# State-space heads: the state product for two heads at once, and an order of VectorE and ScalarE work around it

## What is computed

```python
    cb = jnp.einsum('bclgn,bcsgn->bcgls', c_c, b_c)
    y_diag = jnp.einsum('bcgjls,bcsgjp->bclgjp', cb[:, :, :, None] * decay, xdt)
    states = jnp.einsum('bclgn,bclgjp->bcgjpn', b_c, xdt * decay_to_end[..., None])
    # prev: the states passed on from chunk to chunk
    decay_from_start = jnp.exp(a_cs).transpose(0, 1, 4, 2, 3)
    y_off = jnp.einsum('bclgn,bcgjpn->bclgjp', c_c, prev) * decay_from_start[..., None]
    y = (y_diag + y_off).reshape(bsz, n_chunks * SSD_CHUNK, SSD_D_INNER)[:, pad:]
    y = y + xs.astype(f32) * jnp.repeat(d_skip.astype(f32), SSD_HEAD_DIM)
```

## Time and profile before

| | us |
|---|---|
| median of 3 runs | 2684.39 |
| lowest and highest | 2682.53, 2685.54 |
| profiled execution, own time | 2682.57 |
| its span, first to last instruction | 2680.8 |
| PE busy | 2585.4 (96%) |
| DVE busy | 1276.8 (48%) |
| ScalarE busy | 994.2 (37%) |
| POOL busy | 934.8 (35%) |

### The profile page before, as it was taken

The page is one execution under the profiler, slowest core; times in us unless marked ns, Lnnn a source line. Parts: engine busy times, 40 slices in busy tenths (PEclk is TensorE's granted clock), DMA queues, the critical chain, the costliest instruction groups (busy, mean ns, idle before and its releaser), DMA issues.

```text
span 2680.8 us, 36115 instructions
## 1 busy us (share of the span) xinstructions
PE 2585.4 (96%) x15112; PEld 2229.1 (83%) x15112; DVE 1276.8 (48%) x1729; ACT 994.2 (37%) x1520; POOL 934.8 (35%) x382
## 2 busy tenths in 40 slices
PE   7999999899999998899999999999997999999999
PEld 5777777677777787799999899999995887788887
DVE  6454452264454415788888543211235776522211
ACT  3333333343333334244454423322334565333321
POOL 3344344334334342222333234344432001344443
PEclk9999999999999999899999999999998999999999
DMA  4233233223333331212212123223221000233332
GB/s 138 89 99 103 89 106 91 75 84 110 89 98 106 94 95 47 63 56 64 64 58 62 49 86 100 89 87 95 87 75 56 17 17 25 70 111 94 94 96 87
DMA packets 61329, 215.66 MB, mean 80 GB/s; under 512 B 8176, under 2 KB 8560, under 8 KB 61168
## 3 DMA queue, kind: packets, MB, share of 16 engines
q1 hardware_dynamic: 57248, 202.05, 25.2%
q10 hardware_dynamic: 3920, 11.31, 1.3%
...
## 4 chain that ended last, share of the span: by engine, by line
PE 88%; DVE 7%; ACT 2%; issue 2%; DMA 1%; POOL 0%; DVEq 0%; ACTq 0%
PE psum L379 75%; PE psum L473 1%; PE psum L483 1%; PE psum L670 1%; PE psum L961 1%; PE psum L995 1%; PE psum L673 1%; PE psum L391 1%; PE psum L625 1%; DMA sb_w_raw<-in_weights 1%; DVE sb_cdec L2000 1%; PE psum L959 1%; PE psum L978 1%; PE psum L934 1%; DVE sb_scale L1577 1%
## 5 line engine op out<-in xcount | busy, mean ns | idle before, releaser
L353 POOL TENSOR_TENSOR sb_w_lo<-sb_w_raw,sb_w_hi 128x1024 fp32r<-128x1024 f32 x377 | 933.6, 2479 | 1718.5 <-ACT sb_w_hi L1115 1718.5
L379 PE MATMUL psum<-sb_h_hi,sb_w_hi 128*128 128x512 f32 (+1 forms) x2648 | 818.5, 351 | 48.1 <-DVE sb_h_lo L1586 32.3
L379 PE MATMUL psum<-sb_h_lo,sb_w_hi 128*128 128x512 f32 (+1 forms) x2648 | 795.7, 342 | 0.0
L379 PE MATMUL psum<-sb_h_hi,sb_w_lo 128*128 128x512 f32 (+1 forms) x2648 | 792.8, 341 | 0.0
L1115 ACT ACTIVATE sb_w_hi<-sb_w_raw 128x1024 fp32r<-128x1024 f32 x377 | 395.8, 1055 | 605.5 <-PE psum L379 455.2
L379 PEld LDWEIGHTS psum<-sb_h_hi,sb_w_hi 128*128 128x128 f32 x2648 | 459.8, 191 | 121.3 <-issue 32.7
L379 PEld LDWEIGHTS psum<-sb_h_lo,sb_w_hi 128*128 128x128 f32 x2648 | 458.8, 190 | 60.3 <-issue 4.4
L379 PEld LDWEIGHTS psum<-sb_h_hi,sb_w_lo 128*128 128x128 f32 x2648 | 459.0, 191 | 56.3
L379 PE MATMUL psum<-sb_mix_hi,sb_w_hi 128*128 128x264 f32 (+1 forms) x1424 | 417.8, 339 | 10.3 <-POOL sb_w_lo L353 5.6
L379 PE MATMUL psum<-sb_mix_lo,sb_w_hi 128*128 128x264 f32 (+1 forms) x1424 | 412.1, 335 | 0.0
L379 PE MATMUL psum<-sb_mix_hi,sb_w_lo 128*128 128x264 f32 (+1 forms) x1424 | 410.8, 334 | 0.0
...
## 6 DMA issues: line engine op xcount, KB each, us to landing
...
```

What stands on the lines that cost most here:

```text
L353: e.tensor_tensor(g.w_lo[:, u % 4, :], g.w_raw[:, u % 2, :], g.w_hi[:, u % 4, :].bitcast(F32), ALU.subtract).then_inc(S["w_lo"], 1)
L379: mm = e.matmul(g.psum[0:m, at + b, 0:wd], w[:, slot, P * i:P * i + m], xs[:, tile, c:c + wd], start=first and n == 0, stop=last and n == 2)
```

## The change

- `pe_ssd_a` runs once for two heads: the first head's rows go to partitions 0 to 63, the second's to 64 to 127, from position Q = 88 on. There are four instructions, of 176 and 264 columns for each head, of 64 weights.
- New `pe_ssd_state_y`: for two heads at once, the states of the pair (128 columns of `state` as weights) by C itself, five products of 88 columns. It is done beside unit 0 after seven of its eight blocks, and beside unit 2 after four. It waits for the states, the second time for `skip`.
- `pe_ssd_y` keeps only `xdt` by `part`; it waits for `state_y`.
- New `act_ssd_decays_from_start`: the exponential into `cdec`, once for a pair; for the second pair it comes after the norm's `act_rsqrt` beside head 1.
- New `dve_ssd_state_y`: `cdec` times the product in PSUM, then `xs` times the scalar plus that, into the group's output for positions 88 on. `dve_ssd_skip` is now two instructions: the first 88 positions as before, and for the others a sum of output and PSUM. DVE no longer multiplies by C (L2000).
- `pe_ssd_mask` of odd heads waits for the exponentials of the head before.
- Order on DVE: `dve_ssd_skip` of the first pair beside head 1, weights of head 2 behind the first tap of conv 1, the second state product behind its second tap, weights of head 3 ahead of the low parts and of conv 2. In the last group the low parts come ahead of the weights of head 3.
- Order on ScalarE: the split beside head 0 comes ahead of that head's decays; the one beside head 1 behind the second exponential of the pair.

The names of the new semaphores in the list SIGNALS are left out here.

```diff
@@ -627,25 +627,42 @@
     mm.then_inc(S["states_sum"], 1)
 
 
-def pe_ssd_a(g, e, grp, h):
-
-    S = g.S
-    n = HG * grp + h
-    if h == 0:
+def pe_ssd_a(g, e, grp, c):
+
+    S = g.S
+    n = HG * grp + 2 * c
+    if c == 0:
         e.wait_ge(S["bt2"], grp + 1)
     else:
         e.wait_ge(S["decay2"], n)
-    for half in range(2):
-        mm = e.matmul(g.flat(6 * 512 + 248 + HALF * half, HALF), g.sel[0:96, n:n + 1].to_broadcast([96, P]),
-                      g.rows[0:96, HALF * half:HALF * half + HALF], start=True, stop=True)
+    for h in range(2):
+        by, rows = g.sel[0:96, n + h:n + h + 1].to_broadcast([96, 64]), slice(64 * h, 64 * h + 64)
+        e.matmul(g.flat(6 * 512 + 248 + Q, HALF - Q)[rows], by, g.rows[0:96, Q:HALF], start=True, stop=True)
+        mm = e.matmul(g.flat(7 * 512, HALF)[rows], by, g.rows[0:96, HALF:L], start=True, stop=True)
     mm.then_inc(S["a_row"], 1)
 
 
+def pe_ssd_state_y(g, e, grp, c):
+
+    S = g.S
+    if c == 0:
+        e.wait_ge(S["state"], STEPS_OF_STATE * (grp + 1))
+    else:
+        e.wait_ge(S["skip"], 2 * grp + 1)
+    for j in range(1, NC):
+        mm = e.matmul(g.flat(4 * 512 + 248 + Q * j, Q), g.state[:, j - 1, P * c:P * c + P],
+                      g.ct[:, grp % 2, Q * j:Q * j + Q], start=True, stop=True)
+    mm.then_inc(S["c_state"], 1)
+
+
 def pe_ssd_mask(g, e, grp, h):
 
     S = g.S
     n = HG * grp + h
-    e.wait_ge(S["decay1"], n + 1)
+    if h % 2 == 0:
+        e.wait_ge(S["decay1"], n // 2 + 1)
+    else:
+        e.wait_ge(S["decay2"], n)
     for half in range(2):
         e.matmul(g.flat(6 * 512 + 248 + HALF * half, HALF)[0:Q], g.sel[0:96, n:n + 1].to_broadcast([96, Q]),
                  g.rows[0:96, HALF * half:HALF * half + HALF], start=True, stop=False)
@@ -659,19 +676,12 @@
 
     S = g.S
     n, row = HG * grp + h, 64 * (h % 2)
-    if h == 0:
-        e.wait_ge(S["state"], STEPS_OF_STATE * (grp + 1))
-    if h == 2:
-        e.wait_ge(S["skip"], 2 * grp + 1)
+    if h % 2 == 0:
+        e.wait_ge(S["state_y"], 2 * grp + h // 2 + 1)
     e.wait_ge(S["weighted"], n + 1)
-    e.wait_ge(S["c_dec"], n + 1)
     for j in range(NC):
-        out = g.flat(4 * 512 + 248 + Q * j, Q)[row:row + 64]
-        mm = e.matmul(out, g.xdt[0:Q, j, 64 * h:64 * h + 64], g.part[0:Q, h % 2, Q * j:Q * j + Q],
-                      start=True, stop=j == 0)
-        if j:
-            mm = e.matmul(out, g.state[:, j - 1, 64 * h:64 * h + 64],
-                          g.cdec[:, h % 2, Q * (j - 1):Q * j], start=False, stop=True)
+        mm = e.matmul(g.flat(4 * 512 + 248 + Q * j, Q)[row:row + 64], g.xdt[0:Q, j, 64 * h:64 * h + 64],
+                      g.part[0:Q, h % 2, Q * j:Q * j + Q], start=True, stop=True)
     mm.then_inc(S["y_part"], 1)
 
 
@@ -755,12 +765,23 @@
                 pe_ssd_out(g, e, h, 0, range(4))
             else:
                 pe_ssd_out(g, e, h - 2, 1, range(3))
-            if h < HG - 1:
-                pe_ssd_a(g, e, grp, h + 1)
+            if h == 0:
+                if not last:
+                    pe_ssd_unit(g, e, grp + 1, 0, range(4, 7))
+                else:
+                    pe_ssd_out(g, e, 0, 0, range(4, 7))
+                pe_ssd_state_y(g, e, grp, 0)
+                rest = range(7, 8)
+            else:
+                rest = range(4, 8)
+            if h == 1:
+                pe_ssd_a(g, e, grp, 1)
+            elif h == 2:
+                pe_ssd_state_y(g, e, grp, 1)
             if not last:
-                pe_ssd_unit(g, e, grp + 1, h, range(4, 8))
+                pe_ssd_unit(g, e, grp + 1, h, rest)
             elif h < 2:
-                pe_ssd_out(g, e, h, 0, range(4, 8)).then_inc(S["unit"], 1)
+                pe_ssd_out(g, e, h, 0, rest).then_inc(S["unit"], 1)
             else:
                 pe_ssd_out(g, e, h - 2, 1, range(3, 6))
             if h == 0 and grp:
@@ -1277,17 +1298,26 @@
         act_ssd_squares_high(g, e, grp - 1)
 
 
+def act_ssd_decays_from_start(g, e, grp, c):
+
+    S = g.S
+    e.wait_ge(S["a_row"], 2 * grp + c + 1)
+    if grp:
+        e.wait_ge(S["with_skip"], 2 * (grp - 1) + c + 1)
+    e.activation(g.cdec[:, c, :], g.flat(6 * 512 + 248 + Q, L - Q), ACT.Exp).then_inc(S["decay1"], 1)
+
+
 def act_ssd_decays(g, e, grp, h):
 
     S = g.S
     n = HG * grp + h
-    e.wait_ge(S["a_row"], n + 1)
-    if n >= 2:
-        e.wait_ge(S["y_part"], n - 1)
     at = 6 * 512 + 248
     if n == 0:
         e.wait_ge(S["dt_v"], DT_ALL)
-    e.activation(g.cdec[:, h % 2, :], g.flat(at + Q, L - Q), ACT.Exp).then_inc(S["decay1"], 1)
+    if n >= 2:
+        e.wait_ge(S["y_part"], n - 1)
+    if h == 0:
+        act_ssd_decays_from_start(g, e, grp, 0)
     if h == 2 and grp:
         act_ssd_high(g, e, grp - 1)
     e.wait_ge(S["masked"], n + 1)
@@ -1315,11 +1345,15 @@
     for grp in range(GROUPS):
         e.preload_act_table_set("natural_log_exp_and_others")
         for h in range(HG):
+            if h == 0:
+                act_split(g, e, U_SSD + GROUP * (grp + 1) + LEAD)
             act_ssd_decays(g, e, grp, h)
-            if grp < GROUPS - 1 or h < HG - 1:
+            if h == 1:
+                if grp:
+                    act_rsqrt(g, e, rs_group(grp - 1), g.mean[:, 0:L], g.rinv[:, 0:L])
+                act_ssd_decays_from_start(g, e, grp, 1)
+            if h and (grp < GROUPS - 1 or h < HG - 1):
                 act_split(g, e, U_SSD + GROUP * (grp + 1) + h + LEAD)
-            if h == 1 and grp:
-                act_rsqrt(g, e, rs_group(grp - 1), g.mean[:, 0:L], g.rinv[:, 0:L])
         act_ssd_silus(g, e, grp + 1)
         if grp < GROUPS - 1:
             act_ssd_setup(g, e, grp + 1)
@@ -1923,28 +1957,26 @@
                     ALU.mult).then_inc(S["z_in"], 1)
 
 
-def dve_ssd_conv(g, e, grp, i):
+def dve_ssd_conv(g, e, grp, i, parts=range(4)):
 
     S = g.S
     ch = (16 + grp, 24 + grp, 2 * grp, 2 * grp + 1)[i]
     out, n = ssd_channels(g, grp, i), 4 * grp + i + 1
-    if i == 0 and grp:
-        e.wait_ge(S["cb_sum"], grp)
-    if i == 1 and grp >= 2:
-        e.wait_ge(S["c_dec"], HG * (grp - 1))
-    e.wait_ge(S["dt_v"], 1)
-    e.wait_ge(S["lifted"], n)
-    e.tensor_scalar(out, g.lift[:, i % 2, 3:3 + L], g.col("ssd_conv", 4 * ch + 3),
-                    g.col("ssd_bias", ch), ALU.mult, ALU.add).then_inc(S["tap2"], 1)
-    e.wait_ge(S["tap2"], 3 * n - 2)
-    e.scalar_tensor_tensor(out, g.lift[:, i % 2, 2:2 + L], g.col("ssd_conv", 4 * ch + 2), out,
-                           ALU.mult, ALU.add).then_inc(S["tap2"], 1)
-    e.wait_ge(S["tap2"], 3 * n - 1)
-    e.scalar_tensor_tensor(out, g.lift[:, i % 2, 1:1 + L], g.col("ssd_conv", 4 * ch + 1), out,
-                           ALU.mult, ALU.add).then_inc(S["tap2"], 1)
-    e.wait_ge(S["tap2"], 3 * n)
-    e.scalar_tensor_tensor(out, g.lift[:, i % 2, 0:L], g.col("ssd_conv", 4 * ch), out,
-                           ALU.mult, ALU.add).then_inc(S["conv2"], 1)
+    for part in parts:
+        if part == 0:
+            if i == 0 and grp:
+                e.wait_ge(S["cb_sum"], grp)
+            if i == 1 and grp >= 2:
+                e.wait_ge(S["c_state"], 2 * (grp - 1))
+            e.wait_ge(S["dt_v"], 1)
+            e.wait_ge(S["lifted"], n)
+            e.tensor_scalar(out, g.lift[:, i % 2, 3:3 + L], g.col("ssd_conv", 4 * ch + 3),
+                            g.col("ssd_bias", ch), ALU.mult, ALU.add).then_inc(S["tap2"], 1)
+        else:
+            e.wait_ge(S["tap2"], 3 * n - 3 + part)
+            mm = e.scalar_tensor_tensor(out, g.lift[:, i % 2, 3 - part:3 - part + L],
+                                        g.col("ssd_conv", 4 * ch + 3 - part), out, ALU.mult, ALU.add)
+            mm.then_inc(S["tap2" if part < 3 else "conv2"], 1)
 
 
 def dve_ssd_xdt(g, e, grp, c):
@@ -1994,27 +2026,42 @@
 
     S = g.S
     n = HG * grp + h
-    part, cdec = g.part[0:Q, h % 2, :], g.cdec[:, h % 2, :]
-    e.wait_ge(S["decay1"], n + 1)
-    e.wait_ge(S["silu"], 4 * grp + 2)
-    e.tensor_tensor(cdec, cdec, g.ct[:, grp % 2, Q:L], ALU.mult).then_inc(S["c_dec"], 1)
+    part = g.part[0:Q, h % 2, :]
     e.wait_ge(S["decay2"], n + 1)
     e.wait_ge(S["cb"], grp + 1)
     e.tensor_tensor(part, part, g.cbd[0:Q, :], ALU.mult).then_inc(S["weighted"], 1)
 
 
-def dve_ssd_skip(g, e, grp, c):
-    S = g.S
-    e.wait_ge(S["y_part"], HG * grp + 2 * c + 2)
+def dve_ssd_state_y(g, e, grp, c):
+
+    S = g.S
+    n = 2 * grp + c + 1
+    cdec = g.cdec[:, c, :]
+    e.wait_ge(S["c_state"], n)
+    e.wait_ge(S["decay1"], n)
+    e.tensor_tensor(cdec, cdec, g.flat(4 * 512 + 248 + Q, L - Q), ALU.mult).then_inc(S["state_y"], 1)
+    e.wait_ge(S["state_y"], n)
+    e.wait_ge(S["silu"], 4 * grp + 3 + c)
     if grp >= 2:
         e.wait_ge(S["mix2"], 2 * grp - 2)
-    e.scalar_tensor_tensor(g.group_out(grp, c), g.xs[:, 2 * grp + c, :], g.col("ssd_d", 2 * grp + c),
-                           g.flat(4 * 512 + 248, L), ALU.mult, ALU.add).then_inc(S["skip"], 1)
```

(37 more changed lines are left out.)

6 lines of the change are left out of this document (3 added, 3 removed).

## The result

| | before | after |
|---|---|---|
| median, measured side by side, us | 2682.53 | 2666.61 |
| lowest and highest (5 runs each) | 2676.48, 2685.54 | 2665.25, 2669.11 |
| ratio after / before | | 0.9948, interval 0.9937 to 0.9958 |
| profiled execution, own time | 2682.57 | 2668.83 |
| its span | 2680.8 | 2667.0 |

The change makes the kernel 0.52% faster by the ratio, 13.9 us of 2682.5. The two medians lie 15.9 us apart, the spans of the two profiled executions 13.8. I had forecast 5.0 us, just inside "no change", with a range down to 2671.5.

The account below looks back on a forecast made before the run. PE's instructions were taken as the bound, DVE close behind. First setup -0.4, group 0 +0.4, groups 1 to 6 4.2, last group 0.8: 5.0 us off 2684.4, giving 2679.4; range 2671.5 to 2686, the forecast's own 2677.6 to 2682.

Parts of the forecast that it names:

- What bounds the kernel: State-space group loop: PE's instructions set the time, 52.18 us a group; DVE follows with some 5 us of room.
- The states' product: PE: 160 products of 128x64 become 80 of 128x128 at 0.11 us an instruction; gain 7.0 us, 0.87 a group.
- The decays' rows: PE, `pe_ssd_a`: 0.96 us a group becomes 0.8 plus 0.6 for the 64-partition form; loses 0.44 a group.
- The 0.3 for entering and leaving: PE, `pe_ssd_a`: writing 64 partitions costs 0.3 us each time to enter and leave, two times a group, 0.6.
- The parallel halves: PE: the second head's decay rows run beside the first's; 3.2 us less than forecast, 2676.2; chance 0.05.
- The wait for the weights: PE at head 2's weighted part: recurring wait, 3.5 us in six times, goes; 0.58 in each of groups 1 to 6.
- The walk on DVE and POOL: One group's DVE order with POOL's holds: gate(0) at 41.0, PE waits 0.4 us, gain 0.7 a group.
- PE's side of the walk: PE through one group: loop ends at 33.2, unit 4, b_turn and cb at 40.6, then 0.4 us wait for gate(0).
- The last group: Last group: PE still waits 1.4 us for the low parts, so its gain is PE's own, 0.8 us.
- Rival A: PE alone decides, DVE's gate and xdt come in time: 6.8 us gained, 2677.6, band 2671.5 to 2677.6; chance 0.3.
- Rival C: Second state product on PE waits 1.8 us for skip(0), held by POOL: slower, 2693.8 us; chance 0.1.
- Rival B: DVE and POOL take the whole gain, another DVE instruction caught by POOL, 1.2 us: band 2682 to 2687; chance 0.2.

Follow-up runs that it names:

- a_wide: Changed kernel with the decays' rows of two heads from one 128-column selector, two instructions instead of four, no 64-column form: 2663.25 us, ratio 0.993.

## Why the prediction was wrong, point by point

- **What bounds the kernel** was right: PE's own instructions, with a small recurring wait. After the change it is PE alone. (The prediction reads 45.4, 24.3 and 15.5 for DVE, ScalarE and POOL where the earlier trace rows has 45.5, 24.5 and 15.6; nothing rests on it.)
- **The states' product** was right. PE's timeline of the kernel after has ten instructions in 1.24 us, and one takes 0.27, so they follow one another by (1.24 - 0.27) / 9 = 0.11, as estimated from the earlier trace rows; in the chain the ten take 1.08. In 16 places that is 17.3 us against 24.6: 7.3 gained (7.0 forecast).

```profile
1272.56 1.24 PE L653 MATMUL psum<-sb_ct,sb_state 128*128 128x88 f32 x10
```

- **The decays' rows: the first step that failed.** The step "by column count 4 x (0.08 + 0.12) = 0.8" put four instructions in a row which in fact run two by two. `pe_ssd_a` was charged at 1.4 a group and takes 0.98 (2 x 0.49), against 0.96 before. The loss of 0.44 a group was 0.02. The 0.3 for entering and leaving that I read from the earlier trace rows was real: a_wide gave 0.29 a pair back. What was wrong is the 0.8 for the instructions themselves, 0.4 a pair where two wide ones take 0.20. This term was mis-sized by 0.42 x 8 = 3.4 us. The parallel halves stood among the rivals at 3.2 us and a chance of 0.05, and that chance was too small: I had a stated rule for it and no row against it.
- **The wait for the weights** went, as forecast: 3.5 us. Each of two parts of the change works on it: the split moved alone in the kernel before leaves 1.2 of the 3.5, and the kernel after with the split late has none of it.
- **The walk on DVE and POOL: the second step that failed.** It had gate(0) 0.4 after PE wanted it, and thereby a period set by DVE. The gate came 0.8 before. DVE's timeline of the kernel after, in the order of the walk:

```profile
1267.64 0.70 DVE L2008 TENSOR_TENSOR sb_state<-sb_state,sb_fall 128x256 f32<-128x256 f32 x1
...
1273.84 0.61 DVE L2042 TENSOR_TENSOR sb_cdec<-sb_cdec,psum 128x440 f32<-128x440 f32 x1 [1.69 <-PE psum L653]
...
1282.03 3.45 DVE L2096 SCALAR_TENSOR_TENSOR sb_y<-sb_y,sb_cols,sb_rinv 128x528 f32<-128x528 f32 x2
1285.40 0.29 DVE L2056 SCALAR_TENSOR_TENSOR sb_scaled<-sb_xs,sb_cols,psum 128x88 f32<-128x88 f32 x1
1285.62 0.60 DVE L2058 TENSOR_TENSOR sb_scaled<-sb_scaled,psum 128x440 f32<-128x440 f32 x1
```

  Counted from the mask product's end, 1267.61: the state is complete at 3.9 (walk 4.4), because POOL holds L2008 for 0.3 and not 0.8; the normed output is done at 17.9 (18.9), the skip at 18.6 (19.8), the gatings at 38.9 (40.3), the gate at 39.6 (41.0). The holds were all found where the walk had them (L2096 3.45 for two, L2047 2.12, L2104 3.53), and the order of events was right. The walk was 0.5 us late by the state's end and 1.4 at the gate, an error of 3% over 41 us. But what it had to tell was 0.4 against -0.8, so it could not. It cost the forecast 0.3 a group, 1.8 us in groups 1 to 6. PE's side of the walk has a slip too: from the loop's end at 33.2, unit 4, b_turn and cb take 6.09 + 0.55 + 0.94 = 7.6 us in the chain before, which gives 40.8 and not 40.6, and a wait of 0.2 and not 0.4. Measured, PE wanted the gate at 40.35.
- **The last group** gained 1.2 and not 0.8, with the same wait for the low parts (1.3).
- **The sum.** By the measured terms: 7.3 for the product, 0 for the rows, 3.5 for the wait are 10.8 of the 11.5 us of the stage. A wait of 0.3 us ahead of L670 in the first group is gone too, and the one for the low parts fell from 1.44 to 1.27; some 0.2 stay unassigned. The forecast had 5.0: 3.4 short by the rows, 1.8 by DVE, the rest roundings. A further 2.3 us of the profiled span come from behind the stage, and 1.7 of these go with the clock.
- **The range** ended at 2671.5. Rival A in full, with the halves in parallel, was what happened, and its own numbers (6.8, and 3.2 for the halves) already give 2684.4 - 10.0 = 2674.4. What lies below are 1.5 us more within the stage, the 2.3 outside, which no part of the prediction had, and the few us by which the medians of before differ from one measurement to the next (2679.51 to 2684.39).
- **Rival C** (the wait for the skip) did not happen, but it is what the order of DVE's instructions keeps off: with the order of before, the same product makes the kernel some 30 us slower than after, and slower than before. **Rival B** was nearer than it looked: one instruction of 0.69 us more on DVE at one place, seven times, turns into 22 us.
